# First stage by blocks of tokens, and a bias table begun later, in an encoder block on one core

## What is computed

```python
h = rmsnorm(x, g_mix)        # x * rsqrt(mean(x*x) + eps) * g_mix
proj = h @ w_in              # 1024 x 3584: qa, ka, va, qb, kb, vb, gate_a, gate_b
```

## Time and profile before

| | us |
|---|---|
| median of 3 runs | 1557.87 |
| lowest, highest | 1557.63, 1560.72 |
| the profiled execution's own time | 1560.19 |
| its span | 1558.4 |

### The profile page before, as it was taken

One profiled execution on the slowest core, in us unless ns is written; L12 is line 12 of the kernel. 1 busy time (PEld: TensorE's weight loads), 2 busy tenths in 40 slices (PEclk: granted clock), 3 DMA queues, 4 the chain that ended last, 5 costly groups with the idle time before them and its releaser, 6 DMA issues.

```text
span 1558.4 us, 21231 instructions
## 1 busy us (share of the span) xinstructions
PE 1516.6 (97%) x7254; PEld 1242.8 (80%) x7287; DVE 1310.4 (84%) x1018; ACT 1085.7 (70%) x1155; POOL 259.7 (17%) x170
## 2 busy tenths in 40 slices
PE   7999999996999999999999999999999999999997
PEld 5888778886788888888888888888888888888884
DVE  4456587656799999999999999999999999999975
ACT  4344587224777777777788777777777877778762
POOL 6402245400001200111000000011000000001211
PEclk9999999997999999999999999999999999999997
DMA  8330001535999999999999999999999999999972
GB/s 299 122 105 31 1 1 55 206 135 192 373 372 382 384 393 389 380 389 367 385 389 386 387 384 382 395 386 382 372 383 385 389 387 384 388 388 379 389 259 97
DMA packets 131103, 477.36 MB, mean 306 GB/s; under 512 B 9721, under 2 KB 10241, under 8 KB 130977
## 3 DMA queue, kind: packets, MB, share of 16 engines
q1 hardware_dynamic: 118720, 435.45, 72.4%
q0 software_dynamic: 9936, 36.44, 8.7%
q10 hardware_dynamic: 2416, 5.07, 0.9%
HBM read 452.81 MB, written 24.12 MB: 306 GB/s over the span
## 4 chain that ended last, share of the span: by engine, by line
PE 95%; DVE 2%; ACT 1%; issue 0%; DMA 0%; ACTq 0%; SPq 0%; DVEq 0%
PE ps L1446 28%; PE ps L1448 28%; PE ps L1447 28%; PE ps L1715 2%; PE ps L1723 2%; PE ps L1742 2%; PE ps L1494 2%; PE ps L1537 1%; PE ps L1538 1%; PE ps L1479 1%; PE ps L1667 0%; PE ps L1511 0%; PE ps L1512 0%; DMA xs<-in_x 0%; PE ps L1769 0%
## 5 line engine op out<-in xcount | busy, mean ns | idle before, releaser
L1279 DVE TENSOR_TENSOR chunk_lo<-chunk,chunk_hi 128x2048 fp32r<-128x2048 f32 x384 | 858.8, 2283 | 39.5 <-ACT chunk_hi L886 36.4
L886 ACT ACTIVATE chunk_hi<-chunk 128x2048 fp32r<-128x2048 f32 x378 | 722.5, 1914 | 109.5 <-PE ps L1448 109.0
L1446 PE MATMUL ps<-chunk_hi,XT 128*128 128x512 f32 x1024 | 404.9, 395 | 2.0 <-DVE XT L1324 2.0
L1448 PE MATMUL ps<-chunk_hi,XT 128*128 128x512 f32 x1024 | 400.2, 391 | 0.0
L1447 PE MATMUL ps<-chunk_lo,XT 128*128 128x512 f32 x1024 | 400.0, 391 | 0.0
L660 POOL DMA_INDIRECT sum_rows<-y,idx x31 | 91.9, 2964 | 942.0 <-ACT y L992 887.7
L1446 PEld LDWEIGHTS ps<-chunk_hi,XT 128*128 128x128 f32 x1024 | 192.8, 188 | 41.1 <-DVE XT L1324 2.4
L1448 PEld LDWEIGHTS ps<-chunk_hi,XT 128*128 128x128 f32 x1024 | 192.5, 188 | 40.5
L1447 PEld LDWEIGHTS ps<-chunk_lo,XT 128*128 128x128 f32 x1024 | 192.9, 188 | 38.9
L1446 PE MATMUL ps<-chunk_hi,hidT 128*128 128x512 f32 x512 | 200.3, 391 | 0.0
L1447 PE MATMUL ps<-chunk_lo,hidT 128*128 128x512 f32 x512 | 200.1, 391 | 0.0
(11 more groups left out here) (274 smaller groups left out, 1927.3 us busy)
## 6 DMA issues: line engine op xcount, KB each, us to landing
chunk<-in_w_gate_up SPq DMA_DIRECT2D x256, 1024.0 KB, 8.4
chunk<-in_w_down SPq DMA_DIRECT2D x128, 1024.0 KB, 6.9
raw<-in_w_in SPq DMA_DIRECT2D x14, 1024.0 KB, 7.3
xs<-in_x SPq DMA_DIRECT2D x8, 512.0 KB, 5.2
w_out<-in_w_out SPq DMA_DIRECT2D x4, 1024.0 KB, 6.7
raw<-in_w_branch_a SPq DMA_DIRECT2D x2, 1024.0 KB, 4.9
raw<-in_w_branch_b SPq DMA_DIRECT2D x2, 1024.0 KB, 6.1
sum_rows<-xs ACTq DMA_DIRECT2D x4, 512.0 KB, 2.6
```

What stands on the lines that cost most here:

```text
L886: a.activation(chunk_hi[hi_slot(c, nxt)][:, :], chunk[c][:, :], ACT.Copy).then_inc(ex_hi, 1)
L1279: v.tensor_tensor(chunk_lo[c][:, :], chunk[c][:, :], chunk_hi[hi_slot(c, nxt, first)][:, :].bitcast(F32), ALU.subtract).then_inc(ex_lo, 1)
L1446: mm(dst, lhsT(0), rhs(0), start=start, stop=False)
L1448: return mm(dst, lhsT(1), rhs(0), start=False, stop=stop)
```

## The change

1. SyncE issues x's block 0, chunk 0, block 1, chunk 1, blocks 2 and 3, and then chunks 2 and 3.
2. The norm's weight goes from `hT` into the weights' parts, since each row of `w_in` belongs to one feature: ScalarE makes the upper part by `top_part` with scale `gcol`, four instructions of 128x512 for a chunk, and VectorE the rest by `rest_part`, four SCALAR_TENSOR_TENSOR in place of one TENSOR_TENSOR. This holds for all 14 chunks. The first two chunks give their semaphore after each half, hence `split_parts`.
3. A block of tokens is transposed into two banks of its own (4 and 5, or 6 and 7), and `hT` is made by block: one instruction of 128x1024 on ScalarE, one on VectorE. TensorE transposes block 0 first, and block n+1 in the middle of product n.
4. TensorE issues 8 unread products (bf16, of zeros, into bank 3) before the first transposes and 7 behind them.
5. The five DMAs of constants on ScalarE's queue move behind chunk 2's upper part.
6. GpSimd begins its operations on the bias table only when VectorE has done five chunks (`split_parts(5)`).

```diff
@@ sync @@
-            for n in range(CHUNKS - 2):
-                if n >= NIN:
-                    sp.wait_ge(in_lo, n - NIN + 1)
+            load_x(0)
+            load_chunk(0)
+            load_x(1)
+            load_chunk(1)
+            load_x(2)
+            load_x(3)
+            load_chunk(2)
+            load_chunk(3)
+            for n in range(NIN, CHUNKS - 2):
+                sp.wait_ge(in_lo, split_parts(n - NIN + 1))
                 load_chunk(n)
@@ gpsimd @@
+        def split_parts(n):
+            return n + min(n, 2)
             pool.wait_ge(bias_in, 48)
+            pool.wait_ge(in_lo, split_parts(5))
@@ scalar @@
+            def top_part(n, kk):
+                cols = slice(kk * 512, kk * 512 + 512)
+                k = n % 2 * 4 + kk
+                return a.activation(split[:, n % NIN_SPLIT, 0, cols], raw[:, n % NIN, cols], ACT.Copy,
+                                    scale=gcol[:, k:k + 1])
-                a.activation(split[:, n % NIN_SPLIT, 0, :], raw[:, n % NIN, :], ACT.Copy).then_inc(in_hi, 1)
+                for kk in range(4):
+                    last = top_part(n, kk)
+                last.then_inc(in_hi, 1)
+            def hT_round(c):
+                act.wait_ge(hT_ps, c + 1)
+                a.activation(hT[:, 0, :, c * 128:(c + 1) * 128],
+                             ps[:, 4 + c % 2 * 2:6 + c % 2 * 2, :].rearrange("p t (k n) -> p (t k) n", n=128),
+                             ACT.Copy).then_inc(hT_hi, 1)
+            mix_root(0)
+            first_in_hi(0, 0)
+            hT_round(0)
+            first_in_hi(0, 1)
+            mix_root(1)
+            first_in_hi(1, 0)
+            first_in_hi(1, 1)
+            hT_round(1)
+            mix_root(2)
+            hT_round(2)
+            mix_root(3)
+            hT_round(3)
+            in_split_hi(2)
+            act.dma_start(rp, rope.rearrange("(c p) t n -> p c t n", p=128)).then_inc(consts_in, 16)
...
@@ vector @@
+            def rest_part(n, kk):
+                cols = slice(kk * 512, kk * 512 + 512)
+                k = n % 2 * 4 + kk
+                return v.scalar_tensor_tensor(out=split[:, n % NIN_SPLIT, 1, cols], in0=raw[:, n % NIN, cols],
+                                              scalar=gcol[:, k:k + 1],
+                                              in1=split[:, n % NIN_SPLIT, 0, cols].bitcast(F32), op0=ALU.mult,
+                                              op1=ALU.subtract)
+            mix_norm(0)
+            first_in_lo(0, 0)
+            hT_rest(0)
+            first_in_lo(0, 1)
+            mix_norm(1)
+            first_in_lo(1, 0)
+            first_in_lo(1, 1)
+            hT_rest(1)
+            mix_norm(2)
+            hT_rest(2)
+            mix_norm(3)
+            hT_rest(3)
+            in_split_lo(2)
@@ tensor @@
+            def mix_turn(c):
                 pe.wait_ge(xn_ready, c + 1)
+                if c >= 2:
+                    pe.wait_ge(hT_lo, c - 1)
                 for k in range(KD):
+                    last = t_.transpose(ps[:, 4 + c % 2 * 2 + k // 4, k % 4 * 128:k % 4 * 128 + 128],
+                                        xn[:, c, k * 128:(k + 1) * 128], ident[:, :])
+                last.then_inc(hT_ps, 1)
+            def unread(n):
+                for _ in range(n):
+                    mm(ps[:, 3, :], zeros[:, 0:64].bitcast(BF16), zeros[:, 0:256].bitcast(BF16), start=True, stop=True)
+            pe.wait_ge(zero_set, 1)
+            unread(8)
+            mix_turn(0)
+            unread(7)
...
+                        if n < 3 and k == 4:
+                            mix_turn(n + 1)
+                        if n < 4 and k == 0:
+                            pe.wait_ge(hT_lo, n + 1)
+                        if n == 0 and k % 2 == 0:
+                            pe.wait_ge(in_lo, k // 2 + 1)
+                        elif c == 0 and k % 4 == 0:
+                            pe.wait_ge(in_lo, split_parts(m + 1))
```

More of the change, by code:

```diff
@@ L403, in _, with load_x @@
             x_v = x.rearrange("b (c p) n -> (b c) p n", p=128)
-            for c in range(NT):
+            def load_x(c):
                 sp.dma_start(xs[:, c, :], x_v[c]).then_inc(x_in[c], 16)
@@ L686, in _, with mix_root @@
             a.activation(warm[:, :], eps[:, :], ACT.Sqrt)
-            for c in range(NT):
+            def mix_root(c):
                 act.wait_ge(x_in[c], 16)
@@ L693, in _, with first_in_hi @@
                              scale=1.0 / D).then_inc(rt_done, 1)
[L694 to L698, removed]
+            def top_part(n, kk):
[3 more added lines that the diff above has]
+                                    scale=gcol[:, k:k + 1])
+            def first_in_hi(n, half):
+                act.wait_ge(chunk_in[n], 16)
+                if n + half == 0:
+                    act.wait_ge(gcol_ready, 1)
+                for kk in (2 * half, 2 * half + 1):
+                    last = top_part(n, kk)
+                last.then_inc(in_hi, 1)
             def in_split_hi(n):
@@ L709, in in_split_hi @@
                     act.wait_ge(proj_ps, 4 * (m // 2) + 4)
-                a.activation(split[:, n % NIN_SPLIT, 0, :], raw[:, n % NIN, :], ACT.Copy).then_inc(in_hi, 1)
[L712 to L719, removed]
+                for kk in range(4):
+                    last = top_part(n, kk)
+                last.then_inc(in_hi, 1)
+            def hT_round(c):
[17 more added lines that the diff above has]
+            act.dma_start(rp, rope.rearrange("(c p) t n -> p c t n", p=128)).then_inc(consts_in, 16)
+            act.dma_start(gains[:, 0, :], qa_norm[0:1, :].to_broadcast([128, HD])).then_inc(consts_in, 16)
+            act.dma_start(gains[:, 1, :], ka_norm[0:1, :].to_broadcast([128, HD])).then_inc(consts_in, 16)
+            act.dma_start(sink[:, :], sink_b[0:1, :].to_broadcast([128, 8])).then_inc(consts_in, 16)
+            act.dma_start(brt[:, :], b_router[0:1, :].to_broadcast([128, E])).then_inc(consts_in, 16)
             def project_out(n):
@@ L796, in _ @@
             act.wait_ge(xn_ready, NT)
-            act.wait_ge(hT_ps, KD)
+            act.wait_ge(hT_ps, NT)
             for grp in range(6):
@@ L831, in _ @@
             project_out(25)
-            act.wait_ge(in_lo, IN_CHUNKS)
+            act.wait_ge(in_lo, split_parts(IN_CHUNKS))
             for i in range(3):
@@ L1058, in link, with in_split_lo, first_in_lo, mix_norm @@
                 dve.wait_ge(dve_step, steps[0])
-            for c in range(NT):
+            def rest_part(n, kk):
[5 more added lines that the diff above has]
+                                              op1=ALU.subtract)
+            def in_split_lo(n):
+                if n >= IN_CHUNKS:
+                    return
+                dve.wait_ge(in_hi, split_parts(n + 1))
+                for kk in range(4):
+                    last = rest_part(n, kk)
+                last.then_inc(in_lo, 1)
+            def first_in_lo(n, half):
+                dve.wait_ge(in_hi, 2 * n + half + 1)
+                for kk in (2 * half, 2 * half + 1):
+                    last = rest_part(n, kk)
+                last.then_inc(in_lo, 1)
+            def mix_norm(c):
                 dve.wait_ge(rt_done, c + 1)
@@ L1064, in _, with hT_rest @@
                 v.tensor_scalar(xn[:, c, :], xs[:, c, :], rstd[:, c:c + 1], None, ALU.mult).then_inc(xn_ready, 1)
[L1065 to L1085, removed]
+            def hT_rest(c):
+                dve.wait_ge(hT_hi, c + 1)
+                cols = slice(c * 128, c * 128 + 128)
+                v.tensor_tensor(hT[:, 1, :, cols],
+                                ps[:, 4 + c % 2 * 2:6 + c % 2 * 2, :].rearrange("p t (k n) -> p (t k) n", n=128),
+                                hT[:, 0, :, cols].bitcast(F32), ALU.subtract).then_inc(hT_lo, 1)
+            dve.wait_ge(gcol_ps, 1)
+            v.tensor_copy(gcol[:, :], ps[:, 7, 0:KD]).then_inc(gcol_ready, 1)
+            mix_norm(0)
[11 more added lines that the diff above has]
+            in_split_lo(2)
             for n in range(NIN_SPLIT, 7):
@@ L1452, in _ @@
             t_.transpose(ps[:, 7, 0:KD], g16[0:KD, :], ident[0:KD, 0:KD]).then_inc(gcol_ps, 1)
-            pe.wait_ge(gcol_ready, 1)
-            for c in range(NT):
+            def mix_turn(c):
                 pe.wait_ge(xn_ready, c + 1)
+                if c >= 2:
+                    pe.wait_ge(hT_lo, c - 1)
                 for k in range(KD):
-                    last = t_.transpose(ps[:, k, c * 128:(c + 1) * 128], xn[:, c, k * 128:(k + 1) * 128], ident[:, :])
-                    if c == NT - 1:
-                        last.then_inc(hT_ps, 1)
+                    last = t_.transpose(ps[:, 4 + c % 2 * 2 + k // 4, k % 4 * 128:k % 4 * 128 + 128],
[8 more added lines that the diff above has]
+            unread(7)
             def turn_in(kind, n):
@@ L1558, in _ @@
                     for k in range(KD):
[L1559 to L1562, removed]
+                        if n < 3 and k == 4:
+                            mix_turn(n + 1)
```

(8 more changed lines are left out.)

## The result

The changed kernel takes 1563.98 us in the median of 8 runs (1563.44 to 1565.25), against 1558.55 us for the kernel before in the 8 runs beside it: a ratio of 1.0027, 95% interval 1.0016 to 1.0038. It is slower by 5.4 us; 1564.5 was forecast. The profiled execution took 1564.08 us with a span of 1562.3. The changed kernel was run in this set alone.

What follows compares the result with a forecast made beforehand. TensorE, busy for 97% of the span, was taken as the bound, so early shifts carry to the end. −5.8 + 1.0 + 8.8 + 2.6 = +6.6 us, added to the median 1557.87, gave 1564.5 us; own range 1561.5 to 1569.5.

Steps and rivals of the forecast that it cites:

- the term that decides: In the first stage, GpSimd's bias-table operations come between VectorE's four parts of chunk 5: a TensorE stall of 8.8 us.
- (a): At chunk 5, VectorE keeps its turn through its four parts: stall 1.2 us, no clock loss, 1554.3 us; chance 0.14.
- (b): At chunk 5, the parts don't block at all, or GpSimd's work is past: −4.8 us, 1553.1 us; chance 0.10.
- (c): At the start the clock isn't held up: block 0's products partly at 0.43, 2 to 4 us more, 1567.5; chance 0.08.
- (d): The start is no earlier, as block 0's chain waits for chunk 1's landing: up to 3 us, 1567; chance 0.08.
- The start: Before the first product and in group 0: block 0's norm and transposes come first, 5.8 us earlier, 2.7 of it half clock.
- Chunk 3: Early in group 1: ScalarE reaches chunk 3 late, after the constants' DMAs and three outputs; stall 1.0 us, between 0 and 2.
- Chunk 5: At product 8: three GpSimd operations come between VectorE's four parts, done at 71.1, wanted at 62.3; stall 8.8 us.
- The clock: After the chunk 5 stall: TensorE's idleness lets the clock fall to half; 2.6 us, between 1.7 and 3.4.
- The odd chunks after 5: Chunks 7 to 13: four parts add 0.2 us on ScalarE and 0.4 on VectorE, leaving 0.4 to spare, no cost.
- three operations fit between the parts: At chunk 5: whatever the phase, three GpSimd operations, at least 7.9 us, come between the parts; stall bounds 7 and 10.5.

## Why the prediction was right, point by point

The mechanism that it named as the term that decides is the one that the trace shows, and four runs tell it from its rivals: the table held back, begun early, late in the kernel before, and one instruction for a chunk. Of the prediction's own rivals, (a) and (b) fall by parts 2 and 3, each of which waits for an operation of GpSimd; (c) and (d) by the first product, at 11.45 and at full clock. The sum, +6.6 us, came out 1.2 too high by the medians and 2.2 by product 27. Its terms erred by more than that, both ways: that the result lies so near the forecast is in part luck.

- **The start** (forecast −5.8, first product at 11.7, end of group 0 at 36.8). Measured 11.45, and −6.30 at product 3's output, with group 0 ended by 36.33.
- **Chunk 3** (forecast a stall of 1.0 us). Measured 0.3: product 4's output follows product 3's by 5.78 us, where 5.44 is usual. The step that failed put ScalarE's five DMAs in series behind chunk 2's upper part. They were issued from 28.14 on, beside ScalarE's rounding and splits already in its queue, and chunk 3's upper part began at 33.67, not at 35.8, with a wait for TensorE before it:

```profile
28.14 0.43 ACTq L755 DMA_DIRECT2D shared<-rope_tables  x1
...
33.67 2.56 ACT L711 ACTIVATE split<-raw,gcol 128x512 fp32r<-128x512 f32 x4 [0.62 <-PE ps L1513]
```

  The 2.44 us in the earlier trace rows were idle time in a place where nothing was queued.
- **Chunk 5** (forecast 8.8 us, bounds 7 and 10.5). Measured 6.6, below the lower bound. Two things were mis-sized. The prediction took the 4.91 us of GpSimd's first operation for its time alone. It is 2.80 us, and in the kernel before 2.1 us of waiting came on top, since VectorE had begun chunk 2 just before it:

```profile
25.71 2.29 DVE L1075 TENSOR_TENSOR split<-raw,split 128x2048 fp32r<-128x2048 f32 x1 [1.14 <-ACT split L710]
```

  VectorE's row ends at 28.00, and 2.80 more give 30.8; the row of 4.91 ends at 30.65. With nothing beside it GpSimd was 2.1 us further on than forecast: only the last subtraction and a cast still lay ahead when part 1 was done. And the bound "three operations fit between the parts" took for granted that three were left. The turns themselves went as read from the earlier trace rows, part by part. (The forecast's own terms add up to 71.5 and not 71.1, a stall of 9.2; and its range, from its own parts, to +4.5 and +12.1 us, 1562.4 to 1570.0.)
- **The clock** (forecast 2.6 us). 11 products in 4.73 us, less 11 × 0.227: 2.2 us. The run with unread products in the wait confirms it with 2.2.
- **The odd chunks after 5** (forecast: 0.4 us to spare). Measured 0.35 us late, four times: +1.4. The term that failed is ScalarE's four parts, taken at 2.1 us and lasting 2.56; VectorE's 2.74 was as taken. In the changed kernel:

```profile
86.60 2.56 ACT L711 ACTIVATE split<-raw,gcol 128x512 fp32r<-128x512 f32 x4 [2.06 <-PE ps L1513]
...
89.20 2.74 DVE L1104 SCALAR_TENSOR_TENSOR split<-raw,gcol,split 128x512 fp32r<-128x512 f32 x4 [6.02 <-ACT split L711]
```

From ScalarE's start to VectorE's end these are 5.34 us, where the earlier trace rows have 4.24: the 1.0 us to spare is used up, and the window of 5.4 holds the engines' hand-overs too, for which the forecast left nothing. A run of four without waits between is no cheaper for ScalarE than the earlier trace rows's four with waits (2.40).

So −6.3, +0.2 for chunk 3 (0.3 less the 0.1 that it cost before), +9.05 for chunk 5 with its clock and +1.4 give +4.4, the difference at product 27. The lock on the memory port that the prediction cited from the Trainium skill ("SBUF — State Buffer", the section "SBUF: two separate sides") is borne out for GpSimd's casts and subtractions: part 2 waited 3.9 us for a subtraction whose turn came before it. For GpSimd's TENSOR_SCALAR it isn't: besides, VectorE's chunk 2 took its usual 2.29 us at 26.44 in the run with the constants moved, in the middle of that operation (24.37 to 27.18). The rule on transposes and the clock doesn't agree with the earlier trace rows, nor with that same run. There TensorE did 32 transposes in 5.82 us and nothing else of size, rested, and its first products were at full clock, 0.23 us apart; only from 18.83 on were they at half:

```profile
17.21 0.50 PE L1446 MATMUL ps<-split,hT 128*128 128x512 f32 x1 [4.05 <-DVE hT L1081]
...
18.24 0.40 PE L1447 MATMUL ps<-split,hT 128*128 128x512 f32 x1
...
18.83 0.63 PE L1446 MATMUL ps<-split,hT 128*128 128x512 f32 x1
```

## What to carry to other kernels

Where two engines take turns on a resource for whole instructions, cutting one's work into n pieces lets in up to n − 1 of the other's: count those, by their own lengths, and not the work. Delay the other engine's chain up to a given gap only if the whole chain fits there, or stop it before the next critical piece; a single wait at the sixth of eight operations was worth 7 to 8 us here. And an instruction cut in four for a scale of its own lengthens a hand-over that had 1 us to spare; pass such a chunk on by halves.

## What was not expected of the hardware

- A row's duration can hold another engine's work, in both directions. GpSimd's first operation on the bias table took 4.91 us beside VectorE's chunk 2 and 2.80 to 2.81 in all the other executions. In the run with the constants moved chunk 2 came later and met the cast behind it, which took 3.23 us instead of 1.89. Before a duration is used as a time alone, look at what the other engine did in it.
- The time at which the clock rises is not the same in executions of the same code. In the changed kernel's profiled one the 8 first transposes took 1.21 us, but in that of the run with the table held back 1.97, with the same code up to there:

```profile
7.25 1.97 PE L1526 MATMUL ps<-ident,xn 128*128 128x128 f32 x8 [0.78 <-DVE xn L1129]
9.01 3.01 PE L1532 MATMUL ps<-zeros 128*128 128x512 bf16 x7
11.64 0.61 PE L1513 MATMUL ps<-split,hT 128*128 128x512 f32 x1
```

The unread products ran at half speed there too, and the first product came 0.2 us later than in the changed kernel. In the runs with that beginning the 8 transposes took 1.97 us three times and 1.09 to 1.10 three times. Product 4's output started between 41.57 and 42.59, apart from the run with the early table, and in the kernel before at 48.18, 46.83 and 46.87. So the gain of the start differs by a microsecond or more from one pair of executions to another.
